# Turning an expert's last group between two down pieces, with two homes for turned groups

## The reference

```python
def swiglu(h, w_gu, w_down):
    g, u = jnp.split(h @ w_gu, 2, axis=-1)
    return (jax.nn.silu(g) * u) @ w_down

for e in range(N_EXPERTS):
    y = y + gate[..., e:e + 1].astype(h.dtype) * swiglu(h, w_gu[e], w_down[e])
```

## Time and profile before

| | us |
|---|---|
| median of three runs | 1406.52 (1405.21 to 1407.21) |
| profiled execution, its own time | 1408.91 |
| its span, first to last instruction | 1407.1 |
| TensorE matmul busy | 1354.4 (96%) |
| VectorE busy | 1043.0 (74%) |
| ScalarE busy | 889.2 (63%) |
| mean granted clock of TensorE | 0.980 of full speed |

### The profile page before, as it was taken

The page is one execution under the profiler, slowest core; times in us unless marked ns, Lnnn a source line. Parts: engine busy times, 40 slices in busy tenths (PEclk is TensorE's granted clock), DMA queues, the critical chain, the costliest instruction groups (busy, mean ns, idle before and its releaser), DMA issues.

```text
span 1407.1 us, 19257 instructions
## 1 busy us (share of the span) xinstructions
PE 1354.4 (96%) x7175; PEld 1185.9 (84%) x7175; DVE 1043.0 (74%) x956; ACT 889.2 (63%) x931; POOL 83.1 (6%) x67
## 2 busy tenths in 40 slices
PE   5999989999989999878999999999999999999997
PEld 5889978888978899776898888988988888889886
DVE  3786466544457775655889889898898898988984
ACT  5576546443446755435777777686777776877773
POOL 0320000000002200000000000000000000000000
PEclk9999999999999999978999999999999999999999
DMA  6643345655545423486999999999999999999992
GB/s 226 213 120 120 120 150 173 216 183 169 176 150 192 141 91 133 161 320 228 335 364 382 376 382 380 382 368 390 375 382 374 380 380 379 373 387 374 375 360 61
DMA packets 180525, 381.35 MB, mean 271 GB/s; under 512 B 8650, under 2 KB 63476, under 8 KB 180468
## 3 DMA queue, kind: packets, MB, share of 16 engines
q1 hardware_dynamic: 175248, 369.12, 73.5%
q0 software_dynamic: 2304, 8.39, 2.3%
q10 hardware_dynamic: 2916, 3.07, 0.7%
HBM read 374.27 MB, written 6.29 MB: 270 GB/s over the span
## 4 chain that ended last, share of the span: by engine, by line
PE 88%; ACT 4%; DVE 4%; issue 2%; DMA 1%; ACTq 0%; SPq 0%; POOL 0%; DVEq 0%; POOLq 0%
PE ps L1014 17%; PE ps L1016 17%; PE ps L1015 17%; PE ps L624 8%; PE ps L625 8%; PE ps L626 8%; PE ps L631 2%; PE ps L633 2%; PE ps L632 2%; ACT w_hi L1169 2%; PE ps L1067 1%; DVE w_lo L1507 1%; PE ps L740 1%; PE ps L747 1%; DVE mix L1686 1%
## 5 line engine op out<-in xcount | busy, mean ns | idle before, releaser
L1747 DVE TENSOR_TENSOR w_lo<-mix,w_hi 128x2048 fp32r<-128x2048 f32 (+2 forms) x192 | 394.6, 2067 | 85.0 <-ACT w_hi L1377 84.0
L1377 ACT CAST w_hi<-mix 128x2048 fp32r<-128x2048 f32 (+2 forms) x190 | 329.3, 1737 | 136.8 <-PE ps L1016 136.8
L1014 PE MATMUL ps<-w_hi,eT_hi 128*128 128x512 f32 (+1 forms) x768 | 291.0, 379 | 5.9 <-DVE eT_lo L1889 5.9
L1507 DVE TENSOR_TENSOR w_lo<-raw,w_hi 128x2048 fp32r<-128x2048 f32 (+4 forms) x94 | 198.5, 2119 | 124.4 <-ACT w_hi L1169 123.4
L1015 PE MATMUL ps<-w_lo,eT_hi 128*128 128x512 f32 (+1 forms) x768 | 286.9, 374 | 0.0
L1016 PE MATMUL ps<-w_hi,eT_lo 128*128 128x512 f32 (+1 forms) x768 | 286.5, 373 | 0.0
L1169 ACT CAST w_hi<-raw 128x2048 fp32r<-128x2048 f32 (+4 forms) x94 | 166.4, 1777 | 120.9 <-PE ps L626 107.4
L1747 DVE TENSOR_TENSOR w_lo<-raw,w_hi 128x2048 fp32r<-128x2048 f32 (+1 forms) x96 | 209.5, 2199 | 17.0 <-ACT w_hi L1377 16.6
L1377 ACT CAST w_hi<-raw 128x2048 fp32r<-128x2048 f32 (+1 forms) x96 | 175.3, 1843 | 40.6 <-PE ps L1016 37.7
L1014 PEld LDWEIGHTS ps<-w_hi,eT_hi 128*128 128x128 f32 x768 | 145.4, 189 | 25.4 <-DVE eT_lo L1889 6.0
L1016 PEld LDWEIGHTS ps<-w_hi,eT_lo 128*128 128x128 f32 x768 | 145.2, 189 | 20.6
(11 more groups left out here) (190 smaller groups left out, 1960.3 us busy)
## 6 DMA issues: line engine op xcount, KB each, us to landing
mix<-in_expert_w_gate_up_dram SPq DMA_DIRECT2D x79, 1024.0 KB, 7.5
raw<-in_expert_w_gate_up_dram SPq DMA_DIRECT2D x49, 1024.0 KB, 7.7
mix<-in_expert_w_down_dram SPq DMA_DIRECT2D x49, 1024.0 KB, 8.8
mix<-in_expert_w_gate_up_dram SPq DMA_DIRECT2D x48, 768.0 KB, 8.9
raw<-in_expert_w_down_dram SPq DMA_DIRECT2D x31, 1024.0 KB, 8.0
raw<-in_w_in_dram SPq DMA_DIRECT2D x28, 1024.0 KB, 5.3
raw<-in_dense_w_gate_up_dram SPq DMA_DIRECT2D x16, 1024.0 KB, 5.2
raw<-in_expert_w_gate_up_dram SPq DMA_DIRECT2D x16, 768.0 KB, 8.5
```

What stands on the lines that cost most here:

```text
L1014: pe.matmul(out_, l_hi, w_hi[q][:, cols], start=first, stop=False, skip_group_check=True)
L1377: act.copy(w_hi[q][:, 0:m], e_raw[raw_of(p, first)][:, 0:m]).then_inc(e_hi_ready, 1)
L1507: dve.tensor_tensor(w_lo[q][:, 0:m], raw[u % RAW][:, 0:m], w_hi[q][:, 0:m].bitcast(F32), ALU.subtract).then_inc(split, 1)
L1747: dve.tensor_tensor(w_lo[q][:, 0:m], e_raw[raw_][:, 0:m], w_hi[q][:, 0:m].bitcast(F32), ALU.subtract).then_inc(e_split, 1)
```

## The change

`turn_e` of group 5 is called inside `down_e` of group 4, after its first piece, and no longer after both. VectorE's `hidden_e` for group 5 stands ahead of the split of p = 35, and no longer at p = 0 of the next item behind the first split there, nor in `finish_items` between the two splits. Groups 0, 2, 4 have the first home of `e_hidT`, groups 1, 3, 5 a second one, in the space of `hT_hi`; every reader and writer names the home by j % 2.

```diff
-        e_hidT = [over(f"e_hidT_{n}", [P, 4, CAP], mix_at + 4 * part(4 * CAP)) for n in ("hi", "lo")]
+        e_hidT = [[over(f"e_hidT{b}_{n}", [P, 4, CAP], (hT_at + 16 * CAP * m) if b else (mix_at + 4 * part(4 * CAP)))
+                   for m, n in enumerate(("hi", "lo"))] for b in range(2)]
...
                     last.then_inc(e_used, 1)
+                    if j == FF - 2 and piece == 0:
+                        turn_e(i, FF - 1, first)
...
                     down_e(i, j - 1, first)
-                    turn_e(i, j, first)
+                    if j < FF - 1:
+                        turn_e(i, j, first)
...
-            def turned_high_e(no, blocks):
+            def turned_high_e(no, blocks, b):
                 act.wait_ge(turn_done, no)
-                act.copy(e_hidT[0][:, 0:blocks, :], view(2, blocks, CAP)).then_inc(e_turned_hi, 1)
+                act.copy(e_hidT[b][0][:, 0:blocks, :], view(2, blocks, CAP)).then_inc(e_turned_hi, 1)
...
                     if first and p in (4, 5):
                         continue
+                    if p == PER_ITEM - 1:
+                        hidden_e(i, FF - 1, unit_no(i, p - 2) + 1)
                     if not (first and p < SPLIT):
                         split_low_e(i, p, first)
                     if p == 0:
-                        if not first:
-                            hidden_e(i, -1, i * PER_ITEM - 4)
                         gathered(i)
...
             def finish_items(i):
                 low_of_unit(i * PER_ITEM + (PER_ITEM - 1), raw_of(0, False), split_of(0, False), unit_size(4))
-                hidden_e(i, FF - 1, unit_no(i, up_at(FF - 1) + 3) + 1)
                 low_of_unit(i * PER_ITEM + PER_ITEM, raw_of(1, False), split_of(1, False), unit_size(5))
-                turned_low_e(i * FF + FF, BLOCKS[-1])
+                turned_low_e(i * FF + FF, BLOCKS[-1], (FF - 1) % 2)
```

More of the change, by code:

```diff
@@ L1043, in down_e @@
                             at = (b - lo) * D + half * 512
-                            last = three_e(ps[4 + half][:, :], [part_[:, b, :] for part_ in e_hidT], split_of(p, first),
+                            last = three_e(ps[4 + half][:, :], [part_[:, b, :] for part_ in e_hidT[j % 2]], split_of(p, first),
                                            slice(at, at + 512), j + b == 0, False)
                     last.then_inc(e_used, 1)
+                    if j == FF - 2 and piece == 0:
+                        turn_e(i, FF - 1, first)
             def down_last(i):
@@ L1056, in down_last @@
                             at = (b - lo) * D + half * 512
-                            last = three_e(ps[4 + half][:, :], [part_[:, b, :] for part_ in e_hidT], split_of(p, False),
+                            last = three_e(ps[4 + half][:, :], [part_[:, b, :] for part_ in e_hidT[(FF - 1) % 2]], split_of(p, False),
                                            slice(at, at + 512), False, b == BLOCKS[-1] - 1)
@@ L1120, in finish_items @@
                             at = (b - lo) * D + half * 512
-                            last = three_e(ps[4 + half][:, :], [part_[:, b, :] for part_ in e_hidT],
+                            last = three_e(ps[4 + half][:, :], [part_[:, b, :] for part_ in e_hidT[(FF - 1) % 2]],
                                            split_of(piece, False), slice(at, at + 512), False, b == BLOCKS[-1] - 1)
@@ L1461, in item @@
                     if p == 3 and not first:
-                        turned_high_e(i * FF, BLOCKS[-1])
+                        turned_high_e(i * FF, BLOCKS[-1], (FF - 1) % 2)
                     if p == 9 and not first:
@@ L1465, in item @@
                     if p in turns:
-                        turned_high_e(i * FF + (turns[p] + 1), BLOCKS[turns[p]])
+                        turned_high_e(i * FF + (turns[p] + 1), BLOCKS[turns[p]], turns[p] % 2)
             def finish_items(i):
@@ L1473, in finish_items @@
                     act.copy(w_hi[q][:, 0:m], e_raw[raw_of(piece, False)][:, 0:m]).then_inc(e_hi_ready, 1)
-                turned_high_e(i * FF + FF, BLOCKS[-1])
+                turned_high_e(i * FF + FF, BLOCKS[-1], (FF - 1) % 2)
                 results(i + 1, [i * PER_ITEM + (PER_ITEM - 1), i * PER_ITEM + PER_ITEM])
@@ L1897, in hidden_e, with turned_low_e @@
                 dve.tensor_tensor(e_hid[:, 0:w], e_act[:, 0:w], ps[1][:, 0:w], ALU.mult).then_inc(hid_done, 1)
-            def turned_low_e(no, blocks):
+            def turned_low_e(no, blocks, b):
                 dve.wait_ge(e_turned_hi, no)
-                dve.tensor_tensor(e_hidT[1][:, 0:blocks, :], view(2, blocks, CAP), e_hidT[0][:, 0:blocks, :].bitcast(F32),
+                dve.tensor_tensor(e_hidT[b][1][:, 0:blocks, :], view(2, blocks, CAP), e_hidT[b][0][:, 0:blocks, :].bitcast(F32),
                                   ALU.subtract).then_inc(e_turned, 1)
@@ L1910, in item @@
                     if p == 0:
-                        if not first:
-                            hidden_e(i, -1, i * PER_ITEM - 4)
                         gathered(i)
                     if p == 3 and not first:
-                        turned_low_e(i * FF, BLOCKS[-1])
+                        turned_low_e(i * FF, BLOCKS[-1], (FF - 1) % 2)
                     if p == (8 if first else 6):
@@ L1918, in item @@
                     if p == 9:
-                        turned_low_e(i * FF + 1, BLOCKS[0])
+                        turned_low_e(i * FF + 1, BLOCKS[0], 0)
                     if p > 9 and p % 6 == 0 and p < PER_ITEM:
@@ L1924, in item @@
                     if p > 9 and p % 6 == 3:
-                        turned_low_e(i * FF + p // 6, BLOCKS[p // 6 - 1])
+                        turned_low_e(i * FF + p // 6, BLOCKS[p // 6 - 1], (p // 6 - 1) % 2)
                     if p == 20:
```

## The result

| | before | after |
|---|---|---|
| median of seven runs, us | 1405.21 (1402.68 to 1407.62) | 1414.55 (1410.0 to 1416.29) |
| profiled execution's span, us | 1407.1 | 1414.3 |
| one expert in the loop, us | 94.13 | 95.35 |
| from the start of VectorE's product to the end of `eT_lo`, us | 1.74 (both splits ahead of the product) | 5.09 |
| first down matmul of the last group 4 to first matmul of the end, us | 6.72 | 6.41 |

The changed kernel takes 1.0056 times as long as before, with a 95% interval of 1.0036 to 1.0076. It is slower, by 9.3 us at the medians: a small step, but one that lies clear of the scatter. Of the executions behind the experiments' ratios three stood far from all others, at 1521, 3168 and 5636 us, and are not in them.

The account below looks back on a forecast made before the run. TensorE's own work was taken to bound the expert loop. Seven boundaries at 1.2 us (8.4) less 0.8 at the end gave +7.6 us on 1406.52, so 1414.1 us, range 1410.8 to 1418.0.

Parts of the forecast that it names:

- What bounds the loop: Expert loop: TensorE's own work is the limit, busy for all 94.13 us of an expert and waiting for nobody.
- The sum on VectorE: Expert boundary: product, 1024-column split, split p = 0 and `eT_lo` pair take 5.09 us, so `eT_lo` ends 1.35 us later.
- TensorE's stop: Next expert's first matmul: starts 1.04 to 1.35 us later, 1.2 taken, at each of seven boundaries, 8.4 us in all.
- Parts 2 and 3: Three transposes moved between the down pieces, and a second home for the turned groups: cost 0 each.
- The end: Ahead of the last expert's down products: turned group ready no sooner; gain between 0 and 0.98 us, 0.8 taken.
- the 0.98 us: Time before the end's first matmul put down to nothing visible; perhaps TensorE's way out of the loop, its condition 0.95 earlier.
- The rival that it falls in each pause: Clock drops after each of seven boundary pauses, 1.7 us each, 12 us more: 1426; chance 0.05.
- signs of being wrong: Experts still at 94.13 us, a clock below 1.00 after the pauses, or TensorE waiting on other splits too.
- The total: Whole kernel: 8.4 - 0.8 = +7.6 us, giving 1414.1 us.
- more waits follow: The 1024-column split's whole 2.6 us lateness reaches TensorE at seven boundaries: +17.4 us, 1423.9; chance 0.05.

Follow-up runs that it names:

- experiment 6: The kernel before with TensorE's two loops written as one, the end read from the register; ratio 0.9995 (0.9981 to 1.0009).
- Experiment 5: The changed kernel with the product one split further ahead, in front of the split of p = 34; one execution, 1439.35 us, experts 98.67 us.
- experiment 1: The changed kernel with TensorE's turn of group 5 back behind both down pieces; ratio 1.0056 (1.0037 to 1.0076), experts 95.35 us.
- experiment 2: The changed kernel with VectorE's old order, the turn staying between the down pieces; ratio 1.0020 (1.0008 to 1.0032), experts 94.28 us.
- experiment 3: The homes alone: the kernel before with two homes, both orders as they were; ratio 1.0004 (0.9989 to 1.0020), experts 94.13 us.
- experiment 8: VectorE's order as before, two homes, TensorE's loops as one, group 5 turned between the second down piece's halves; ratio 0.9985 (0.9969 to 1.0000).
- experiment 7: The changed kernel with the product behind the split of p = 35 and TensorE's two loops as one; ratio 1.0000 (0.9989 to 1.0011).

## Why the prediction was right

The time and the loop's mechanism came as forecast. The end did not, and that the totals lie so close is in part luck, as the points on the end and the total say.

- **What bounds the loop.** Right: every us that TensorE lost in the loop stood in the time. With TensorE busy throughout, a delay of another engine costs from the point at which it passes TensorE's supply.
- **The sum on VectorE.** 5.09 us from the product's start to the end of `eT_lo` was forecast; 821.34 to 826.43 is 5.09. The product's start, taken from ScalarE's copy, was right too: 0.27 us after the first down matmul, where the forecast had 823.05 - 822.77 = 0.28.
- **TensorE's stop.** 1.2 was taken between 1.04 and 1.35; an expert grew by 1.22. TensorE starts 0.23 us after `eT_lo` ends (826.43 to 826.66), so most of the 0.36 us in before was not slack. The 1.2 was a choice between the bounds, with register steps as its reason; that it met 1.22 so closely is luck. 7 x 1.22 = 8.5 against 8.4.
- **Parts 2 and 3.** The homes cost nothing, as forecast. The transposes cost nothing in the changed kernel; in the old order of VectorE they cost 0.15 us, which the forecast had no need to say.
- **The end.** The mechanism was right: the turned group is no sooner ready (5.76 against 5.73 us), and the 0.98 us are the way out of the loop, which experiment 6 shows. The size was off: 0.8 us was taken and 0.3 came. The step that failed is that this way would end 0.95 us sooner because its condition did, which takes its length as fixed. By the trace's records of the jump it starts 3.12 us after the first down matmul in before and lasts 3.35; in the changed kernel it starts at 2.26 and lasts 3.91. So its start came 0.86 us sooner, near the forecast, and 0.56 of that went again in the jump. With the same code it took 3.35 to 3.91 us in the seven kernels that have it, 3.75 in the homes alone, where nothing on this path had changed. The end's first matmul there comes 7.12 us after the first down matmul, against 6.72 in before and 6.41 in the changed kernel: the 0.3 us are within what this way varies by itself. Why it varies is open. The Trainium skill, "Runtime: NRT & Kernel Launch", section "Instruction fetch mechanics", has a branch beyond the instructions at hand wait for a page; experiment 6 agrees, as the wait goes when the code that is jumped over goes, but no run here shows the fetch itself.
- **The clock.** The rival that it falls in each pause had 0.05, and in the loop it did not: TensorE's seven pauses had 1.00 behind them. It fell at the end. The forecast has a clock below 1.00 after the pauses among its signs of being wrong, and had excluded it there with one execution's row at 1.00. That is 1.6 us in this profile, about what the medians' 9.3 have over the forecast 7.6. But the ratio of 1.0056 gives 7.9 us, so this match shows nothing, and whether the clock fell in the other executions too isn't known.
- **The total.** In the profiled executions the loop gave +8.5 us (forecast 8.4), the end +1.7 (forecast -0.8, the wrong way), and the stretch ahead of both -3.0, which has nothing to do with the change. That their sum, 7.2, lies by the forecast 7.6 is luck. What carries the forecast is the loop: with 8.5 us from it, an end of -0.8 and one of +1.7 both stay within the range.
- **The rival "more waits follow"** was right to be small: the next splits were in time. Experiment 5 shows what it would have been.

## What to carry to other kernels

On an engine with its own order, an instruction that waits is as expensive as everything behind it that used to run in its shadow. Before an instruction is moved ahead, list what stands between its new and its old place, add their durations from the point where its wait ends, and compare that with what the bounding engine still has to do; here 5.09 against 4.10 us (823.05 to 827.15) decided it, for a gain at the end that could be had once and a loss paid seven times. Where only the last round gains, look for a place for the other engine's step that asks nothing of this one.

## What the runs showed of the hardware

- **Pauses and TensorE's clock.** Stops are given here from the start of one matmul to that of the next, a transpose being one too. With TensorE busy throughout before them, stops of 1.33 to 1.43 us (seven in the changed kernel) left the clock at 1.00, the 2.4 GHz level. Stops of 3.26 us in experiment 5 were followed by the 1.2 GHz level (not yet the first, 3.35 us long, but the seven after it), 0.43 us between matmuls of 512 columns instead of 0.23. At the end, stops between 2.1 and 2.8 us went both ways: the clock fell after 2.16 us in the changed kernel, after 2.14 in experiment 1 and after 2.43 in experiment 2, and stayed after 2.37 in before and 2.77 in experiment 3, whose windows read (first experiment 2's, then experiment 3's):

```profile
1393.00:1398.00 5.00, 4.90 (x15) 3.86 (x16) 0.00 (x0) 0.69 (x1) 0.00 (x0) 0.66 0.01 3
```

```profile
1389.00:1394.00 5.00, 4.07 (x18) 3.30 (x18) 0.00 (x0) 0.69 (x1) 0.00 (x0) 1.00 0.01 3
```

One profiled execution says little of whether such a pause costs 1.6 us.

- **The scatter of whole runs** comes in part from stretches that the kernels share. In the profiled executions the first boundary's `eT_lo` starts at 731.4 (before), 726.6 (experiment 3) and 724.5 (experiment 8), though but for the addresses of the second home nothing ahead of it differs in VectorE's or TensorE's work; that is more than most of the effects studied here. Spans of single executions can't be compared for them, the time of an expert can.
- **Two loops, of which one is never entered,** cost TensorE 0.86 us at the end (experiment 6). The jump itself took 3.35 to 3.91 us in the seven kernels that have it; most of it lay beside matmuls already handed to the array and the wait for the turned group. ScalarE and VectorE jump over such a loop as well; VectorE showed 0.3 us in experiment 7 and ScalarE nothing.
